# Two softmax attentions that transpose unscaled probabilities, a reordered output projection, and operands of a down projection prepared inside the last FFN step

## The reference

```python
fox  = softmax(q.k/8 + c[t] - c[s], causal) @ v     # 8 heads of 64
sb   = stick_breaking(sq, sk, sv)                   # 4 heads of 64
x    = x + concat(fox*silu(fg), pool*silu(pg), sb*silu(sg)) @ w_out
a    = softmax(q2.k2/sqrt(96), causal) @ v2         # 8 heads of 64
m    = concat(rmsnorm(a), rmsnorm(short_conv))
x    = x + rmsnorm(m @ w_out2)
f    = (silu(h @ w_gate) * (h @ w_up)) @ w_down     # 2816 wide
x    = x + rmsnorm(f)
x    = x + sigmoid(x @ w_ple_gate) * rmsnorm(p @ w_ple_proj)
```

## Time and profile before

| | us |
|---|---|
| median of 3 runs | 1018.7 (1015.01 to 1019.91) |
| the profiled execution | 1010.39 |
| its span, first to last instruction | 1008.7 |
| PE busy in the span | 936.6 (93%) |
| DVE busy | 403.5 |
| ACT busy | 333.8 |
| POOL busy | 431.0 |
| mean granted TensorE clock | 0.979 of full |

### The profile page before, as it was taken

One profiled execution on the slowest core, in us unless ns is written; L12 is line 12 of the kernel. 1 busy time (PEld: TensorE's weight loads), 2 busy tenths in 40 slices (PEclk: granted clock), 3 DMA queues, 4 the chain that ended last, 5 costly groups with the idle time before them and its releaser, 6 DMA issues.

```text
span 1008.7 us, 12347 instructions
## 1 busy us (share of the span) xinstructions
PE 936.6 (93%) x4476; PEld 750.5 (74%) x4476; DVE 403.5 (40%) x638; ACT 333.8 (33%) x669; POOL 431.0 (43%) x225
## 2 busy tenths in 40 slices
PE   3999999989997999889889699999999999998997
PEld 3888887655676988766657497888888878887785
DVE  5423363447316175654656761000000011444643
ACT  4132403455303300365543552222222222233531
POOL 7487674120065576550222245443444434443231
PEclk9999999998998999989989799999999999999999
DMA  5142321100022232211110123223223222233112
GB/s 215 56 154 84 107 103 63 43 22 21 1 96 73 83 105 105 83 63 43 42 51 35 63 96 134 91 96 104 85 102 104 83 86 101 86 102 105 43 64 103
DMA packets 23688, 83.08 MB, mean 82 GB/s; under 512 B 2896, under 2 KB 3024, under 8 KB 23648
## 3 DMA queue, kind: packets, MB, share of 16 engines
q1 hardware_dynamic: 22176, 78.65, 22.7%
q10 hardware_dynamic: 1472, 3.88, 1.1%
HBM read 80.39 MB, written 2.10 MB: 82 GB/s over the span
## 4 chain that ended last, share of the span: by engine, by line
PE 47%; issue 30%; POOL 14%; DVE 5%; ACT 2%; DMA 1%; POOLq 1%; SPq 0%; DVEq 0%; ACTq 0%
POOL w_lo L390 14%; PE bank L425 12%; PE bank L427 11%; PE bank L426 11%; PE bank L568 3%; PE bank L482 3%; PE bank L591 2%; PE bank L646 2%; PE bank L636 1%; DVE h L1350 1%; PE bank L659 1%; DMA x<-in_x 1%; DVE h L1506 1%; ACT arena L945 1%; DVE aT_lo L1374 1%
## 5 line engine op out<-in xcount | busy, mean ns | idle before, releaser
L390 POOL TENSOR_TENSOR w_lo<-raw,w_hi 128x1024 fp32r<-128x1024 f32 x142 | 352.1, 2482 | 285.9 <-ACT w_hi L945 280.4
L425 PE MATMUL bank<-w_hi,aT_hi 128*128 128x512 f32 (+4 forms) x600 | 232.0, 387 | 25.6 <-ACT arena L945 5.1
L425 PE MATMUL bank<-aT_hi,w_hi 128*128 128x512 f32 (+1 forms) x600 | 230.4, 384 | 6.3 <-ACT arena L945 3.8
L427 PE MATMUL bank<-aT_hi,w_lo 128*128 128x512 f32 (+1 forms) x600 | 226.8, 378 | 0.0
L426 PE MATMUL bank<-aT_lo,w_hi 128*128 128x512 f32 (+1 forms) x600 | 226.8, 378 | 0.0
L426 PE MATMUL bank<-w_lo,aT_hi 128*128 128x512 f32 (+4 forms) x600 | 226.0, 377 | 0.0
L427 PE MATMUL bank<-w_hi,aT_lo 128*128 128x512 f32 (+4 forms) x600 | 225.7, 376 | 0.0
L385 POOL TENSOR_SCALAR w_hi<-raw 128x1024 fp32r<-128x1024 f32 x66 | 75.5, 1144 | 272.4 <-PE bank L427 252.5
L945 ACT ACTIVATE w_hi<-raw 128x1024 fp32r<-128x1024 f32 x76 | 80.5, 1060 | 249.0 <-PE bank L427 236.3
L425 PEld LDWEIGHTS bank<-w_hi,aT_hi 128*128 128x128 f32 x600 | 115.1, 192 | 48.9 <-issue 10.9
L425 PEld LDWEIGHTS bank<-aT_hi,w_hi 128*128 128x128 f32 x600 | 113.0, 188 | 27.7 <-issue 3.9
(11 more groups left out here) (165 smaller groups left out, 779.6 us busy)
## 6 DMA issues: line engine op xcount, KB each, us to landing
raw<-in_weights SPq DMA_DIRECT2D x142, 512.0 KB, 3.2
x<-in_x SPq DMA_DIRECT2D x4, 512.0 KB, 7.0
y_out<-x SPq DMA_DIRECT2D x8, 256.0 KB, 2.0
g_pre<-in_gains ACTq DMA_DIRECT2D x3, 512.0 KB, 3.2
g_post<-in_gains ACTq DMA_DIRECT2D x3, 512.0 KB, 3.2
arena<-in_pt ACTq DMA_DIRECT2D x1, 512.0 KB, 5.2
wpool<-in_wpool ACTq DMA_DIRECT2D x1, 128.0 KB, 7.3
cols<-in_cols ACTq DMA_DIRECT2D x1, 43.0 KB, 6.2
```

What stands on the lines that cost most here:

```text
L390: nc.gpsimd.tensor_tensor(w_lo[:, s, :], raw[:, r, :], w_hi[:, s, :].bitcast(F32), ALU.subtract).then_inc(w_split, 1)
L425: mm(out, st_hi, mv_hi, start=start, stop=False)
L427: return mm(out, st_lo, mv_hi, start=False, stop=stop)
```

## The change

`turn_probs` waits for the exponential and no longer for the scaled row. DVE no longer scales; it makes one reciprocal of 128 x 4 for each head, into a buffer of 16 columns. Ahead of the values PE makes 8 matmuls for each pair that spread the reciprocals over the pair's partitions, into the other one of banks 6 and 7 (stationary: a column of `erec` read 64 times; moving: the identity), so both banks belong to one pair at a time. `fox_pair` has one more product. `mla_pair` copies the factors to `out_n`, which lies in `g_pre`, and multiplies; ACT's `pair_out` waits for that. The load of `g_pre` by ACT waits until the last pair is through. Of `out2a`, the blocks k = 0 to 2 of row 1 are made ahead of the wait for the last pair. The last two slices of the FFN have code of their own: the last gate and up products alternate block by block, the left operands that come free are refilled by `stage` for slices 0 to 3 of the down projection, and slice 0 takes the row tiles in the order 0, 2, 3, 1, of which only the last waits for the end of the FFN.

```diff
-        erec = sb("erec", [P, 8])
+        erec = sb("erec", [P, 16])
...
+        out_n = view(g_pre, 0, 2, S)
...
                     n = base + m
-                    pe.wait_ge(normed, n + 1)
+                    pe.wait_ge(exped, n + 1)
...
+                    head = base // T + i0
                     pe.wait_ge(pt_made, base + (i0 + 2) * T)
-                    pair = (base // T + i0) // 2
-                    if i0 >= 4:
-                        pe.wait_ge(pv_drained, pair - 1)
+                    pair = head // 2
+                    if i0 >= 2:
+                        pe.wait_ge(pv_drained, pair)
+                    pe.wait_ge(summed, head + 2)
+                    for qb in range(T):
+                        for i in (head, head + 1):
+                            at = 4 * (i % 4) + qb
+                            mm(bank[7 - pair % 2][(i % 2) * HD:(i % 2 + 1) * HD, qb * P:(qb + 1) * P],
+                               erec[:, at:at + 1].broadcast_to([P, HD]), ident[:, :], start=True, stop=True,
+                               skip_group_check=True)
...
-            for k in range(4):
-                if k == 3:
-                    left_ready(1)
-                    pe.wait_ge(pv_drained, (FOX_H + MLA_H) // 2)
+            for t in range(2):
+                for k in range(3):
+                    for g in range(2):
+                        out2a_block(t, g, k)
+            left_ready(1)
+            pe.wait_ge(pv_drained, (FOX_H + MLA_H) // 2)
+            for t in range(T):
                 for g in range(2):
-                    out2a_block(0, g, k)
-            for t in range(T):
-                for g in range(2 if t > 0 else 0):
-                    for k in range(4):
+                    for k in range(3 if t < 2 else 0, 4):
...
+            def ffn_last(f, c):
+                for b in range(2):
+                    s = (CH["ffn"] + b) % SLOTS
+                    pe.wait_ge(w_split, c + b + 1)
+                    if b == 0:
+                        pe.wait_ge(ffn_act, f - 1)
+                    for k in range(KD):
+                        at = slice(k * P, (k + 1) * P)
+                        last = three(bank[b][:, :], w_hi[:, s, at], w_lo[:, s, at], aT_hi[:, k, :], aT_lo[:, k, :],
+                                     start=(k == 0), stop=(k == KD - 1))
+                    last.then_inc(w_used, 1)
+                pe.wait_ge(w_split, c + 4)
+                pe.wait_ge(ffn_act, f)
+                for k in range(KD):
+                    for b in (2, 3):
+                        s = (CH["ffn"] + b) % SLOTS
+                        at = slice(k * P, (k + 1) * P)
+                        last = three(bank[b][:, :], w_hi[:, s, at], w_lo[:, s, at], aT_hi[:, k, :], aT_lo[:, k, :],
+                                     start=(k == 0), stop=(k == KD - 1))
+                        if k == KD - 1:
+                            last.then_inc(w_used, 1)
+                    if k < SLOTS:
+                        last.then_inc(left_free, 1)
             ffn_first()
-            with pe.Fori(1, NF // 2) as i:
+            with pe.Fori(1, NF // 2 - 1) as i:
...
-            def down_step(t, slot, first=False, end=False):
+            ffn_last(NF - 2, CH["down"] - 4)
+            def down_step(t, slot, first=False, end=False, last_t=T - 1):
...
                                  stop=end)
-                    if t == T - 1 and g == 1:
+                    if t == last_t and g == 1:
...
-            def down_block(k, slot, first=False):
+            def down_block(k, slot):
...
                 for t in range(T):
-                    down_step(t, slot, first)
-            pe.wait_ge(ffn_act, NF)
-            for k in range(4):
-                down_block(k, k, k == 0)
+                    down_step(t, slot)
+            pe.wait_ge(staged, 1)
+            pe.wait_ge(w_split, CH["down"] + 1)
+            for t in (0, 2, 3, 1):
+                if t == 1:
+                    pe.wait_ge(ffn_act, NF)
+                down_step(t, 0, True, last_t=1)
+            for k in range(1, 4):
+                down_block(k, k)
...
             def pair_out(pair):
-                act_.wait_ge(pv_done, FOX_H + 2 * pair + 2)
-                out = bank[6 + pair % 2][:, :]
+                act_.wait_ge(mla_out, pair + 1)
+                out = out_n[:, pair % 2, :]
...
             softmax_attention(FOX_H * T, MLA_H, pair_out, out2c_out)
-            act_.wait_ge(h_made, 2 * T)
+            act_.wait_ge(pv_drained, (FOX_H + MLA_H) // 2)
...
             rsqrt(slice(40, 44))
-            def ffn_silu(f, slot, c, first):
+            def stage(k, slot, used=None):
+                if used is None:
+                    act_.wait_ge(left_free, k + 1)
+                else:
+                    act_.wait_ge(w_used, used)
+                copy(aT_hi[:, slot, :].unsqueeze(1), act[:, bass.ds(k, 1), :]).then_inc(stage_hi, 1)
+            def ffn_silu(f, slot, c, first, last=False):
...
                     weights_hi(c + 3, (CH["ffn"] + 2 * slot + 3) % SLOTS, used=c)
+                for k in range(SLOTS if last else 0):
+                    stage(k, k)
...
             act_.dma_start(g_post[:, :], gains_d[4, :, :]).then_inc(g_post_in, 16)
-            with act_.Fori(1, NF // 2) as i:
+            with act_.Fori(1, NF // 2 - 1) as i:
...
-            def stage(k, slot, used):
-                act_.wait_ge(w_used, used)
-                copy(aT_hi[:, slot, :].unsqueeze(1), act[:, bass.ds(k, 1), :]).then_inc(stage_hi, 1)
+            for f in range(2):
+                ffn_silu(NF - 2 + f, f, CH["down"] - 4 + 2 * f, False, last=(f == 1))
...
             act_.wait_ge(ffn_act, NF)
-            for k in range(4):
-                stage(k, k, CH["down"])
...
                             .then_inc(maxed, 1)
-                    if m > 0:
+                    if m > 0 and m % T == 0:
                         n = base + m - 1
-                        kw = ((m - 1) % T + 1) * P
                         dve.wait_ge(exped, n + 1)
-                        own(V.reciprocal(erec[:, n % 8:n % 8 + 1], esum[:, n % 8:n % 8 + 1]))
-                        V.tensor_scalar(P_buf[:, n % 4, 0:kw], P_buf[:, n % 4, 0:kw], erec[:, n % 8:n % 8 + 1],
-                                        None, ALU.mult).then_inc(normed, 1)
+                        if m > 4 * T:
+                            dve.wait_ge(pv_done, (n // T - 4) // 2 * 2 + 2)
+                        V.reciprocal(erec[:, n % 16 - 3:n % 16 + 1], esum[:, n % 8 - 3:n % 8 + 1]).then_inc(summed, 1)
...
                 dve.wait_ge(pv_done, 2 * pair + 2)
+                own(V.tensor_tensor(gate[:, pair, :], bank[7 - pair % 2][:, :], gate[:, pair, :], ALU.mult))
...
             def mla_pair(pair):
-                out = bank[6 + pair % 2][:, :]
+                out = out_n[:, pair % 2, :]
+                dve.wait_ge(pv_done, FOX_H + 2 * pair + 2)
+                own(V.tensor_copy(out, bank[7 - pair % 2][:, :]))
+                V.tensor_tensor(out, bank[6 + pair % 2][:, :], out, ALU.mult).then_inc(mla_out, 1)
...
                 ffn_rows(f, f, CH["ffn"] + 2 * f)
-            with dve.Fori(1, NF // 2) as i:
-                for f in range(2):
-                    ffn_rows(i * 2 + f, f, i * 4 + (CH["ffn"] + 2 * f))
...
-            dve.wait_ge(ffn_act, NF)
+            with dve.Fori(1, NF // 2 - 1) as i:
+                for f in range(2):
+                    ffn_rows(i * 2 + f, f, i * 4 + (CH["ffn"] + 2 * f))
+            ffn_rows(NF - 2, 0, CH["down"] - 4)
...
                 stage(k, k)
+            ffn_rows(NF - 1, 1, CH["down"] - 2)
+            dve.wait_ge(ffn_act, NF)
```

More of the change, by code:

```diff
@@ L293, in hybrid_kernel @@
         angles = sem("angles")
-        scored, maxed, exped, normed = sem("scored"), sem("maxed"), sem("exped"), sem("normed")
+        scored, maxed, exped, summed = sem("scored"), sem("maxed"), sem("exped"), sem("summed")
+        mla_out = sem("mla_out")
         turned, pt_made, pv_done, pv_drained = sem("turned"), sem("pt_made"), sem("pv_done"), sem("pv_drained")
@@ L306, in hybrid_kernel @@
         ffn_gate, ffn_act = sem("ffn_gate"), sem("ffn_act")
-        stage_hi, staged = sem("stage_hi"), sem("staged")
+        left_free, stage_hi, staged = sem("left_free"), sem("stage_hi"), sem("staged")
         p_hi, p_split, emb_made = sem("p_hi"), sem("p_split"), sem("emb_made")
```

## The result

The changed kernel takes **1029.6 us** (median of 4 runs, 1028.21 to 1033.82), the kernel before 1019.3 (4 runs, 1015.01 to 1020.0). The ratio is 1.011, with a 95% interval of 1.0082 to 1.0138: slower, by 8 to 14 us. The forecast was 1025.6, within 1013 to 1034.

The account below looks back on a forecast made before the run. The prediction took PE, busy 936.6 of 1008.7 us, as the bound. Its terms, 8.0 + 2.7 - 1.0 - 1.2 - 1.5 + 4.1 - 4.2 = +6.9 us, added to the median 1018.7 gave 1025.6 us, range 1013 to 1034.

Parts of the forecast that it names:

- The reciprocals on PE: Ahead of each pair's values in both attentions: the added small matmuls cost PE 1.0 us a pair, +8.0 us in all.
- The rival by which the halves don't share PE: At the reciprocal matmuls: column halves or their loads don't overlap, 1.9 us a pair, +7.2, giving 1032.8 us; chance 0.13.
- The first attention otherwise: First attention apart from the reciprocals: the second product and tied-up banks cost nothing, PE's 1.03 us wait stays; 0.
- given back: Waits of PE for ACT in both attentions absorb 6.2 us of the added time, giving 1019.4 us; chance 0.19.
- The second attention: Second attention: ACT waiting inside its queue makes PE stand, +2.7 us; removing DVE's scaling gives -1.0, -1.2 and -1.5.
- The full clock taken back: Second attention's last values: they return from half to full clock, since PE no longer stands for the scaling; -1.5 us.
- the shorter end: End of the second attention: without the scaling, the last values start sooner after the third pair's values; -1.2 us.
- Row 0: Output projection: DVE starts row 0 later, and the whole delay reaches the FFN; +4.1 us.
- FFN to down: Step from FFN to down projection: early staging removes PE's 2.55 us gap and 1.68 us of half clock; -4.2 us.
- not slower, by the clock: Denser attention ends keep the clock up behind the first attention and to the FFN's start; 1015.6 us, chance 0.13.

Follow-up runs that it names:

- the doubled run: The changed kernel with each of the 64 reciprocal matmuls on `erec` made twice; one run of 1034.45 us.
- the staging run: The kernel before with only the change's last part, the FFN's last slices and the staging for the down projection; 1014.7 us, ratio 0.996.

## Why the prediction was right, and where it was not

The direction and the range held; the forecast was 4.0 us too low, and by its parts this is in good part luck.

- *The reciprocals on PE*, 1.0 us a pair: 0.87, so 7.0 us instead of 8.0, which is the lower bound given (0.88). The margin of 0.1 us for a gap behind the group was not needed. The rival by which the halves don't share PE is out, by the trace and by the doubled run. The Trainium skill's rule ("TensorE: Matmul & The Clock Gate", the section "The mechanism" of Part 3), that a weight load overlaps matmuls in flight only where the row groups differ, thus does not hold for these matmuls: 0.87 us is measured, where 1.9 was estimated by it.
- *The first attention otherwise*, 0: right, the waits are the same to 0.01 us. The rival "given back" is out. The 1.7 us by which its last values took longer is clock, which the prediction didn't count; the old code had it too in the staging run's profile (4.07 us).
- *The second attention*, this is **the step that failed**: +2.7 - 1.0 - 1.2 - 1.5 = -1.0 was forecast beside the matmuls, +7.3 measured. The order of events was right to 0.2 us up to the low part. Its duration was mis-sized: "takes 0.7" was read where the operand lay in PSUM, and the change put it in SBUF; 2.18 beside POOL. I had seen the same stretch in `L1506` and booked its removal as a gain, but the change put in its place another instruction that takes longer beside POOL, and a maximum for which PE then waits stands behind it.
- *The full clock taken back* (-1.5, and with it the -1.2 of the shorter end): the last values ran at half clock again, now with the reciprocals ahead of them. By an estimate from the windows the granted clock cost about 6.8 us of the stage after (0.43 x 4 + 0.34 x 5 + 0.18 x 7 + 0.36 x 6) against about 3.4 before (0.82 over 8 us from 515 and 0.61 over 5 from 523). PE's stalls grew by 3.1 (behind the first pair from 1.81 to 3.24, behind the second from 1.10 to 2.44, at the end from 3.76 to 4.11). These two make 6.5 of the 7.3; 0.8 is not placed.
- *Row 0*, +4.1: 4.1 at DVE's row 0, 3.8 at the FFN. Its undoing gave 3.0 at the FFN, and 3.5 with the wait for `g_pre` moved. That the late load of `g_pre` is hidden was right only under the delay: once that is taken away, the load is late next.
- *FFN to down*, -4.2: 4.2 in the trace, 4.1 in a run of its own.
- The rival "not slower, by the clock" was wrong in sign: the rival counted on denser work at the ends of the attentions, but the change thinned PE's work in the second one, and the clock fell more there.

With the sizes measured, the prediction's own terms come to +13.9 us and not +6.9; the ledger's +15.0 holds the 1.7 us at the first attention's end and the -0.5 at the FFN's start besides. The forecast was too low by that. But it worked out its terms against one execution and added them to a median that lies 8.3 us above it, and that execution was an uncommonly fast one: the medians differ by only 10.3. The forecast thus lies near by two errors of opposite sign, and the stage that made most of the loss was forecast with the wrong sign.

## What to carry to other kernels

Follow every moved operand to the duration of its reader, with what its neighbour engine does at that moment: one low part of 0.75 us became 2.18 when it read its operand from SBUF beside POOL, and stood ahead of what PE waited for. Where an in-order engine takes work with a round trip to another engine, put the second half of it later in the queue; here two steps were worth 12 us, the whole loss. And before you take a difference from one profile of each kernel, look at whether the thin places ran at the same clock in both.

## What the runs showed of the hardware

- DVE's low part with both operands in SBUF is not slowed in proportion by POOL's `w_lo`. Begun 0.74 us into it, it took 2.18 us (488.38 to 490.56, POOL's end at 490.01); begun 2.08 us into it, it took 0.83. Both ended 0.54 to 0.55 us behind POOL. Begun 2.33 us into it, 0.05 before POOL's end, it took the 0.75 us that it takes alone. With one operand in PSUM it takes 0.75 us in the midst of POOL's instruction. The scaling that the change removed, with its one large operand in SBUF, was held too: 2.44 us, to 0.14 behind POOL's end.

The low part alone later (first two lines), and the pair's work two steps later (last three):

```profile
492.69 0.83 DVE L1396 SCALAR_TENSOR_TENSOR aT_lo<-g_pre,cols,aT_hi 128x512 fp32r<-128x512 f32 x1
...
490.61 2.37 POOL L392 TENSOR_TENSOR w_lo<-raw,w_hi 128x1024 fp32r<-128x1024 f32 x1
...
493.22 0.75 DVE L1396 SCALAR_TENSOR_TENSOR aT_lo<-g_pre,cols,aT_hi 128x512 fp32r<-128x512 f32 x1 [0.17 <-ACT arena L1220]
...
490.89 2.38 POOL L392 TENSOR_TENSOR w_lo<-raw,w_hi 128x1024 fp32r<-128x1024 f32 x1
493.33 1.54 POOL L387 TENSOR_SCALAR w_hi<-raw 128x1024 fp32r<-128x1024 f32 x1
```

In the last of them POOL's own instruction starts 0.11 us into the low part and takes 1.54 us; the one of its kind ahead of it took 1.04.

- Stalls of 1 to 3 us are followed, in some executions, by windows of 4 to 6 us with a low granted clock, and in others not. It was 0.57 over 4 us behind stalls of 2.00 and 1.00, and 0.66 over 5 us behind 1.19 and 1.01, where the run with doubled reciprocals had 1.00 over 13 us around and behind the same two. Behind one and the same wait of 2.83 us it was 0.57 over 4 us in one execution and 1.00 over 19 us in the other. With stalls of at most 1.10 us it was 1.00 over 45 us. In the second attention this second loss grew by some 3.4 us, as much as the stalls themselves (3.1), and it is what makes two profiles hard to compare.
